# Six transpose banks for the mixed rows, their loads moved up, a stacked state update and later mapped rows in a one-core decoder step

## The chip, the cores and the metric

The kernel runs on one core of one Trainium2 chip. The metric is the device time of one execution in microseconds (us). Before the change it is 1812.33 us, the median of three runs (1810.74 to 1819.49). TensorE multiplies, VectorE (DVE), ScalarE (ACT) and GpSimd (POOL) compute elementwise, SyncE (SP) issues most DMAs, and ACT and POOL issue the others. Each engine works through its own list in order and waits on semaphores.

## What is computed

One layer of a hybrid decoder, for a prompt of 512 tokens and for 8 sequences of 4 new tokens each (32 sample rows). Width 2048.

```python
z = rms_norm(x) @ w_in                 # one projection for all three head groups
m = mLSTM(4 heads x 256)               # prompt and, with a carried state, the 8 sequences
a = sparse attention(4 x 128), keys picked by an indexer, gathered from a paged cache
c = cross-attention(4 x 128) into 256 memory tokens
mix = concat(m * silu(gate), a * silu(gate), c * silu(gate))
y = x + rms_norm(mix @ w_out)
# the carried mLSTM state of each sequence and head (T = 4 tokens):
C_new = a * C + einsum('bhs,bhse,bhsd->bhed', w_s, v, k)      # 256 x 256
n_new = a * n + einsum('bhs,bhsd->bhd', w_s, k)
h = (s @ v + a_inter * C q) / max(|den|, exp(-m_t))
```

## The kernel before

All data are float32. A projection tile is 512 columns wide and is done in 8 chunks. For each chunk ACT copies the weights to a rounded 32-bit half `w_hi`, POOL subtracts to get the rest `w_lo`, and TensorE multiplies three ways (hi by hi, lo by hi, hi by lo; L443 to L445, for the sample rows L431 and L432). A chunk is 28 matmuls of 512 columns. Other work is woven in: each engine's generators are stepped once or twice a chunk ("hosted" pieces). Four parts matter here, in order of time.

**Mapped rows.** For each sample row 256 keys are picked by top-k on DVE (L871 to L873); `vector_physical` (L875) turns them into rows of the paged cache, ending in L892/L893. `tensor_physical` (L904) waits for that (`phys_ready`), transposes the result (L908) and waits until DVE has copied it (L899, `phys_u_ready`). POOL's gathers wait for the same copy. TensorE has this piece behind chunk `MAP_AT` of the main run of tiles; the gathers begin `CK0 = MAP_AT + 2` pieces in.

**The four mLSTM heads.** After the last projection tile `tensor_mlstm_head` runs for h = 0 to 3. Inside a head come four score products (L1754), each followed by `side(0)` and `side(1)`. Beside head 0 that is the preparation of the sample state (L2109, then L2116 on TensorE; `vector_mlstm_s_prep` on DVE). Beside heads 1 to 3 each `side` is one *pair* p (one sample head and one sequence) of `tensor_mlstm_s`; 32 pairs in all, the last 8 run alone behind head 3 (I call them the tail).

**A pair.** On TensorE: the update matmuls (L2150) put v weighed by w times k into `S_UPD`; then S_OUT, the product with the turned state (L2155); then TURN, the four transposes of the next state block (L2132). On ACT: the turned state is copied out of PSUM (L2173, L2174), and S_OUT waits for it. On DVE: `weigh_values` (L2184) for the pair after, then the new state (L2194), for which the next pair's update matmuls wait, since there is one `S_UPD` bank. SP loads state blocks seven pairs ahead (L1979) and stores each new one (L1985). After the eighth pair of a head DVE normalises the output rows (L1854 to L2204), and TensorE waits for L2204.

**The mixed rows.** `mix` lies in DRAM as four blocks of 128 prompt rows and one of 32 sample rows, 2048 wide. Each is loaded (L212), turned on TensorE in groups of four transposes (L284) through the two banks `ps_a` and `ps_b`, taken as `x_hi` by ACT (L304) and as `x_lo` by DVE (L316). There are four groups to a block, 20 in all. Two blocks fit in `y_buf`; SP loads the first two behind the last head (`sync_y_early`), the others when buffers come free. Then comes the output projection (L443 again), the end of the program.

Of the kernel before, what the change touches and what calls it, by code (L numbers as in the profile page):

```python
# [4 lines left out]
def hybrid_decoder_step(nc, I, C, O):  # L5
# [65 lines left out]
    with ctx:  # L71
# [37 lines left out]
        with pro:  # L109
# [16 lines left out]
                        "qs_ready", "ot_copied", "mixed_s", "cmax", "ps_ready", "mixed_c",  # L126
                        "sm_ready", "scv_ready", "ks_scaled", "bc_copied", "qspr_ready", "pws_ready",
# [3 lines left out]
                        "g_exp", "g_ln", "g_we", "g_cols", "cexp", "gate_c_ready", "scv_silu", "sw_exp",),  # L131
# [27 lines left out]
        x_loaded = [sem("x_loaded0"), sem("x_loaded1")]  # L159
        rstd_ready, consts_in = sem("rstd_ready"), sem("consts_in")  # L160
# [39 lines left out]
        def rows_buffer(u):  # L200
            return x_in[:, u % 2, :] if u < NU_NORM else y_in(u)
# [4 lines left out]
        def sync_rows(sp, u0, u1):  # L206
            for u in range(u0, u1):
                if u >= 2:
                    sp.wait_ge(rows_turned, NGRP * (u - 1))
                if 2 <= u < NU_NORM:  # L210
                    sp.wait_ge(squares_done, u - 1)
                sp.dma_start(rows_buffer(u)[0:unit_rows[u], :], unit_source(u)).then_inc(x_loaded[u % 2], 16)  # L212
# [56 lines left out]
        def tensor_turn(pe, u):  # L269
            n = unit_rows[u]  # L270
            pe.wait_ge(x_loaded[u % 2], 16 * (u // 2 + 1))
            for j in range(NGRP):
                g = NGRP * u + j
                if u < NU_NORM:
                    if g >= 2:
                        pe.wait_ge(row_scaled, g - 1)
                else:
                    pe.wait_ge(lo_taken, g - 1)
                if j:
                    yield  # L280
                bank = (ps_a, ps_b)[g % 2]
                for i in range(TG):
                    k = j * TG + i
                    last = nc.tensor.transpose(bank[:, i * n:(i + 1) * n], rows_buffer(u)[0:n, k * P:(k + 1) * P],  # L284
                                               ident[0:n, 0:n])
                last.then_inc(rows_turned, 1)
            yield

        def scalar_take_hi(act, u):
            n = unit_rows[u]  # L290
            if u == NU_NORM:
                act.wait_ge(chunk_used, CH * N_Y0)
                act.wait_ge(sn_out, 32)
                for i in range(NCR):
                    act.wait_ge(cst_out[i], 16 * len(range(i, HB, NCR)))
            for j in range(NGRP):
                g = NGRP * u + j
                if u < NU_NORM:
                    src = turned[:, g % 2, 0:TG * n].rearrange("p (k r) -> p k r", k=TG)
                    act.wait_ge(row_scaled, g + 1)  # L300
                else:
                    src = (ps_a, ps_b)[g % 2][:, 0:TG * n].rearrange("p (k r) -> p k r", k=TG)
                    act.wait_ge(rows_turned, g + 1)
                nc.scalar.copy(unit_dest(u, j * TG, TG)[0], src).then_inc(hi_taken, 1)  # L304
                if j == NGRP - 1 and u < NU_NORM:
                    scalar_square(act, u)
                yield

        def vector_take_lo(dve, u):
            n = unit_rows[u]  # L310
            for j in range(NGRP):
                g = NGRP * u + j
                bank = (ps_a, ps_b)[g % 2][:, 0:TG * n].rearrange("p (k r) -> p k r", k=TG)
# [70 lines left out]
        def scalar_hi(act, n, c, w=TN):  # L384
            j = CH * n + c
            if not (isinstance(n, int) and j < 2):
                act.wait_ge(chunk_used, j - 1)
            scalar_load(act, n, c + 2)
# [1531 lines left out]
        k_ns = rows_of(part(xh_free, XN, [MW]), R)  # L1920
        n_in8 = rows_of(part(xh_free, XN + MW, [H, MD]), NB)
# [8 lines left out]
        assert XT + MD + 3 * H * R <= KT * (S + 2 * R)  # L1930
# [12 lines left out]
        vwb = rows_of(part(w_raw[:, RAWS - 1, :, :].rearrange("p k n -> p (k n)"), 0, [2, MD]), R)  # L1943
# [3 lines left out]
        (sm_in, sconv_out, hist_in, sx_turned, ks_turned, ks_copied, s_gate, s_added, late_in,  # L1947
            ctt, ct_copied, inter_done, vwb_ready, u_done, upd_done, hs_done, sn_done, sn_copied) = (
            sem(n) for n in ("sm_in", "sconv_out", "hist_in", "sx_turned", "ks_turned", "ks_copied", "s_gate",
            "s_added", "late_in", "ctt", "ct_copied", "inter_done", "vwb_ready", "u_done",  # L1950
# [3 lines left out]
        sn_out, hs_out, spread_set = sem("sn_out"), sem("hs_out"), sem("spread_set")  # L1954

        def sync_mlstm_s(sp):
# [5 lines left out]
            sp.wait_ge(s_added, 1)  # L1962
# [37 lines left out]
        def vector_mlstm_s_prep(dve):  # L2000
            half = 5 * MW // 2
            dve.wait_ge(sm_in, 48)
            nc.vector.tensor_tensor(out=s_nat[:, 0:half], in0=s_nat[:, 0:half], in1=s_low, op=ALU.add).then_inc(s_added, 1)
# [29 lines left out]
            yield  # L2033
            dve.wait_ge(*at("bc_copied"))
# [31 lines left out]
        def scalar_mlstm_s_prep(act):  # L2066
# [8 lines left out]
            for u in range(2):  # L2075
                act.wait_ge(ks_turned, u + 1)
                act.wait_ge(sconv_out, 16 * NB)
                nc.scalar.copy(k_ns[:, u * 512:(u + 1) * 512], (S_TURN, S_UPD)[u][0:R, :]).then_inc(ks_copied, 1)
# [4 lines left out]
        def tensor_mlstm_s_prep(pe):  # L2083
# [29 lines left out]
            pe.wait_ge(ks_copied, 2)  # L2113
# [22 lines left out]
        def tensor_mlstm_s(pe):  # L2136
            pe.wait_ge(*at("qspr_ready"))
            pe.wait_ge(spread_set, 1)
            tensor_state_turn(pe, 0)
            for p in range(HB):  # L2140
# [19 lines left out]
                if b == NB - 1:  # L2160
                    pe.wait_ge(upd_done, p + 1)
                    nc.tensor.matmul(S_UPD[0:NB, 0:MD], w_b[:, h, :], k_ns[:, h * MD:(h + 1) * MD],
# [16 lines left out]
        def vector_mlstm_s(dve):  # L2179
            def weigh_values(p):  # L2180
                h, b = p // NB, p % NB
                if p >= 2:
                    dve.wait_ge(u_done, p - 1)
                nc.vector.tensor_scalar(vwb[:, p % 2, :], s_nat[:, 2 * MW + h * MD:2 * MW + (h + 1) * MD],  # L2184
                                        w_b[:, h, b:b + 1], None, ALU.mult).then_inc(vwb_ready, 1)
# [33 lines left out]
        y_in = lambda u: y_buf[:, u % 2, :]  # L2219
        (gp_in, res_in, y_part, y_var, y_std, y_ready, y_out) = (  # L2220
            sem(n) for n in ("gp_in", "res_in", "y_part", "y_var", "y_std", "y_ready", "y_out"))

        def sync_y_early(sp):
# [3 lines left out]
            sync_rows(sp, NU_NORM, NU_NORM + 2)  # L2227
            sp.dma_start(g_post, I["norm_post"][0:1, :].broadcast_to([P, D])).then_inc(gp_in, 16)

        def sync_y_in(sp):  # L2230
            sp.wait_ge(sn_out, 32)
            for i in range(NCR):
                sp.wait_ge(cst_out[i], 16 * len(range(i, HB, NCR)))
            sync_rows(sp, NU_NORM + 2, NU_ALL)
# [20 lines left out]
        def scalar_y(act):  # L2255
            act.wait_ge(y_var, 1)
            nc.scalar.activation(y_root, y_st, ACT.Sqrt).then_inc(y_std, 1)

        def vector_y(dve):
# [25 lines left out]
            nc.vector.tensor_scalar(y_st, y_st, 1.0 / D, RMS_EPS, ALU.mult, ALU.add).then_inc(y_var, 1)  # L2285
            dve.wait_ge(y_std, 1)
# [14 lines left out]
        MAP_AT = 3  # L2301
# [339 lines left out]
```

## Time and profile before

| what | value |
|---|---|
| median of 3 runs | 1812.33 us (1810.74 to 1819.49) |
| the profiled execution, its own time | 1813.49 us |
| its span in the profile | 1811.8 us |
| TensorE busy | 1654.8 us, 91% |
| DVE busy | 826.4 us, 46% |
| ACT, POOL busy | 543.8 us (30%), 677.0 us (37%) |
| the 16 DMA engines | 249.02 MB, mean 137 GB/s |

Times in the profile are microseconds from the start of the span. A row of the timeline is: start, duration, engine, line, operation, output and inputs, count, and in brackets how long the engine had been idle and what released it. The duration of a matmul contains the depth of the pipeline, so matmuls in a row begin closer together than their durations say; the distance between starts is the pace. PEclk is the granted TensorE clock, as a share of 2.4 GHz: 1.00, or 0.50 for 1.2 GHz. A float32 matmul appears as two instructions in the trace (x4 is two matmuls).

### The profile page before, as it was taken

To read this page: it belongs to the slowest core of one execution; us is meant where nothing else is said; L and a number is where in the kernel's file an instruction comes from. 1 tells how busy PE (TensorE), PEld (TensorE's weight loads), DVE (VectorE), ACT (ScalarE), POOL (GpSimd) and SP (SyncE) were. 2 spreads that over 40 slices of the span, in tenths; PEclk is the share of its full clock that TensorE was granted. 3 is DMA by queue.
4 is the path that set the end of the run, shared out by engine and by line. 5 is a ranking of instruction groups with operands and counts; after the bars stand their busy time and mean duration, and the time that the engine had idled before them with its cause. 6 is when DMAs were issued, how large, how long until landed. Compare 5 with 4: busy or idle time off the path is not lost.

```text
span 1811.8 us, 20893 instructions
## 1 busy us (share of the span) xinstructions
PE 1654.8 (91%) x7745; PEld 1255.4 (69%) x7745; DVE 826.4 (46%) x1357; ACT 543.8 (30%) x858; POOL 677.0 (37%) x446
## 2 busy tenths in 40 slices
PE   6899999999999699998999999997849888799995
PEld 4677775577898577786688878776435555477774
DVE  6500010299999555865384347222045445401114
ACT  5512223222222143222423332323223333312221
POOL 3655531133333466674454445322101111033331
PEclk8999999999999799999999999999858789799997
DMA  5545531233234468667353634358734423632222
GB/s 211 165 115 146 158 107 45 64 108 110 90 99 122 163 202 274 197 193 233 107 151 114 203 104 148 117 89 164 241 80 145 129 92 99 236 123 82 81 85 107
DMA packets 143861, 249.02 MB, mean 137 GB/s; under 512 B 32741, under 2 KB 65449, under 8 KB 140485
## 3 DMA queue, kind: packets, MB, share of 16 engines
q10 hardware_dynamic: 66928, 122.86, 23.2%
q1 hardware_dynamic: 60202, 73.02, 12.8%
q0 software_dynamic: 16640, 51.92, 9.8%
q8 instruction: 58, 0.95, 0.2%
q14 instruction: 33, 0.27, 0.1%
HBM read 204.09 MB, written 43.66 MB: 137 GB/s over the span
## 4 chain that ended last, share of the span: by engine, by line
PE 70%; DVE 19%; DMA 5%; ACT 3%; issue 1%; POOL 1%; ACTq 1%; DVEq 0%; SPq 0%; POOLq 0%
PE acc L443 11%; PE acc L445 11%; PE acc L444 11%; DVE arena L872 4%; DVE arena L873 4%; DVE keep L871 4%; PE acc L431 3%; PE acc L432 3%; PE acc L439 3%; PE acc L441 3%; PE ps_c L1068 3%; PE acc L440 3%; PE acc L2150 2%; PE ps_c L2155 2%; DMA w_raw<-in_w_in 2%; PE acc L1765 1%
## 5 line engine op out<-in xcount | busy, mean ns | idle before, releaser
L394 POOL TENSOR_TENSOR w_lo<-w_raw,w_hi 128x1024 fp32r<-128x1024 f32 (+1 forms) x200 | 467.0, 2335 | 805.6 <-ACT w_hi L390 805.4
L443 PE MATMUL acc<-w_hi,x_hi 128*128 128x512 f32 (+1 forms) x1216 | 475.0, 391 | 12.2 <-POOL w_lo L394 11.1
L445 PE MATMUL acc<-w_hi,x_lo 128*128 128x512 f32 (+1 forms) x1216 | 465.5, 383 | 0.0
L444 PE MATMUL acc<-w_lo,x_hi 128*128 128x512 f32 (+1 forms) x1216 | 464.8, 382 | 0.0
L390 ACT CAST w_hi<-w_raw 128x1024 fp32r<-128x1024 f32 (+1 forms) x200 | 204.2, 1021 | 764.1 <-PE acc L432 705.0
L443 PEld LDWEIGHTS acc<-w_hi,x_hi 128*128 128x128 f32 x1216 | 230.3, 189 | 77.4 <-issue 17.6
L445 PEld LDWEIGHTS acc<-w_hi,x_lo 128*128 128x128 f32 x1216 | 229.7, 189 | 45.2
L444 PEld LDWEIGHTS acc<-w_lo,x_hi 128*128 128x128 f32 x1216 | 230.2, 189 | 42.3 <-issue 0.7
L431 PE MATMUL acc<-w_hi,x_hi 128*64 128x512 f32 (+1 forms) x368 | 141.5, 386 | 0.0
L432 PE MATMUL acc<-w_lo,x_hi 128*64 128x512 f32 (+1 forms) x368 | 141.1, 384 | 0.0
L439 PE MATMUL acc<-x_hi,w_hi 128*128 128x512 f32 x256 | 105.3, 411 | 0.0
L441 PE MATMUL acc<-x_lo,w_hi 128*128 128x512 f32 x256 | 100.5, 393 | 0.0
L440 PE MATMUL acc<-x_hi,w_lo 128*128 128x512 f32 x256 | 100.4, 392 | 0.0
L2270 DVE TENSOR_TENSOR arena<-arena (+1 forms) x16 | 14.0, 887 | 177.2 <-ACT arena L476 177.2
L958 POOL DMA_INDIRECT arena<-in_cache_attn_k,keep x64 | 67.1, 1049 | 19.5 <-issue 19.5
L871 DVE MAX8 keep<-arena 32x8 f32<-32x2052 f32 x32 | 73.2, 2286 | 1.1
L872 DVE FIND_INDEX8 arena<-keep,arena 32x8 uint32<-32x2052 f32 x32 | 72.9, 2277 | 0.0
L873 DVE MATCH_REPLACE8 arena<-keep,arena 32x2052 f32<-32x2052 f32 x32 | 72.6, 2268 | 0.0
L958 POOL DMA_INDIRECT arena<-in_cache_attn_v,keep x64 | 66.7, 1043 | 14.4 <-issue 11.0
L432 PEld LDWEIGHTS acc<-w_lo,x_hi 128*64 128x64 f32 x368 | 49.5, 135 | 31.6 <-issue 0.4
L695 DVE COPY head_rows<-ps_c 128x512 f32<-128x512 f32 x1 | 0.7, 694 | 153.0 <-PE ps_b L685 153.0
L431 PEld LDWEIGHTS acc<-w_hi,x_hi 128*64 128x64 f32 x368 | 49.5, 135 | 23.6 <-issue 0.2
(446 smaller groups left out, 2178.9 us busy)
## 6 DMA issues: line engine op xcount, KB each, us to landing
w_raw<-in_w_in ACTq DMA_DIRECT2D x136, 512.0 KB, 3.7
w_raw<-in_w_out ACTq DMA_DIRECT2D x32, 512.0 KB, 3.6
z_prompt<-z_tile ACTq DMA_DIRECT2D x52, 256.0 KB, 2.7
arena<-z_prompt SPq DMA_DIRECT2D x4, 2088.0 KB, 10.6
w_raw<-in_w_mem_kv ACTq DMA_DIRECT2D x16, 512.0 KB, 4.2
arena<-q_sample POOLq DMA_DIRECT2D x32, 256.0 KB, 4.1
w_raw<-in_w_in ACTq DMA_DIRECT2D x16, 300.0 KB, 3.0
x_in<-in_x_prompt SPq DMA_DIRECT2D x4, 1024.0 KB, 5.1
```

The costliest lines, as they stand in the source:

```text
L390: nc.scalar.copy(w_hi[:, c % 2, :, 0:w], w_raw[:, c % RAWS, :, 0:w]).then_inc(chunk_hi, 1)
L394: nc.gpsimd.tensor_tensor(out=w_lo[:, c % 2, :, 0:w], in0=w_raw[:, c % RAWS, :, 0:w], in1=w_hi[:, c % 2, :, 0:w].bitcast(F32), op=ALU.subt ...
L431: nc.tensor.matmul(acc[m][0:2 * R, 0:w], xs, wh, start=first, stop=False)
L432: last = nc.tensor.matmul(acc[m][0:2 * R, 0:w], xs, wl, start=False, stop=end)
L439: nc.tensor.matmul(acc[m][:, :], wh, xh, start=first, stop=False)
L440: nc.tensor.matmul(acc[m][:, :], wl, xh, start=False, stop=False)
L441: last = nc.tensor.matmul(acc[m][:, :], wh, xl, start=False, stop=end)
L443: nc.tensor.matmul(acc[m][:, 0:w], xh, wh, start=first, stop=False)
L444: nc.tensor.matmul(acc[m][:, 0:w], xh, wl, start=False, stop=False)
L445: last = nc.tensor.matmul(acc[m][:, 0:w], xl, wh, start=False, stop=end)
L871: dlink(nc.vector.max(top8, score))
L872: dlink(nc.vector.max_index(sel_idx[:, 8 * i:8 * i + 8], top8, score))
```

## The change

It has three parts.

1. **Mixed rows.** `rows_buffer` gives each of the five blocks a buffer of its own, `turn_bank` turns the groups over six PSUM banks, and a group waits only for the `x_lo` six groups back. SP issues all four prompt blocks in `sync_y_early`, ahead of the post-norm weights, the last state load and the stores of the tail; the sample block follows when its rows are stored. Before the first group TensorE waits for `c_copied` and `hs_done`. ACT's wait for the state stores moves to the second chunk of the first output tile.
2. **State update.** The keys, weighed values and weights are split in a rounded half and a rest, stacked four high on 128 partitions ([hi, hi, lo, lo] against [hi, lo, hi, lo]), so that one rounded matmul over 128 rows gives all four products that the float32 matmul over 32 rows gave. DVE makes the stacks: `vector_split_keys` once, beside head 0, and three instructions instead of one in `weigh_values`. L2116's wait becomes a wait for the split.
3. **Mapped rows.** `MAP_AT` goes from 3 to 5, and the pieces that hang on it move two chunks.

Some semaphores become points of shared ones, with the same order.

```diff
@@ rows_buffer, sync_rows, tensor_turn
-            return x_in[:, u % 2, :] if u < NU_NORM else y_in(u)
+            return x_in[:, u % 2, :] if u < NU_NORM else mix_rows[u - NU_NORM]
+        def turn_bank(u, g):
+            return (ps_a, ps_b)[g % 2] if u < NU_NORM else MIX_BANKS[g % len(MIX_BANKS)]
-                if u >= 2:
+                if 2 <= u < NU_NORM:
                     sp.wait_ge(rows_turned, NGRP * (u - 1))
+            if u == NU_NORM:
+                pe.wait_ge(c_copied, 2 * H)
+                pe.wait_ge(hs_done, H)
-                    pe.wait_ge(lo_taken, g - 1)
+                    pe.wait_ge(lo_taken, g - len(MIX_BANKS) + 1)
@@ vector_mlstm_s_prep, tensor_mlstm_s_prep
+        def vector_split_keys(dve):
+            for u in range(2):
+                cols, bank = slice(u * 512, (u + 1) * 512), (S_TURN, S_UPD)[u]
+                dve.wait_ge(ks_copied, u + 1)
+                hi = k_stack[0:R, cols]
+                nc.vector.tensor_copy(k_stack[R:2 * R, cols], hi)
+                dlink(nc.vector.tensor_tensor(out=k_stack[2 * R:3 * R, cols], in0=bank[0:R, :], in1=hi.bitcast(F32), op=ALU.subtract))
+                last = nc.vector.tensor_copy(k_stack[3 * R:4 * R, cols], k_stack[2 * R:3 * R, cols])
+            last.then_inc(reached("ks_split"), 1)
...
-            pe.wait_ge(ks_copied, 2)
+            pe.wait_ge(*at("ks_split"))
@@ tensor_mlstm_s, vector_mlstm_s
-                    last = nc.tensor.matmul(S_UPD[:, e * MD:(e + 1) * MD], vwb[:, p % 2, e * P:(e + 1) * P],
-                                            k_ns[:, h * MD:(h + 1) * MD], start=True, stop=True)
+                    last = nc.tensor.matmul(S_UPD[:, e * MD:(e + 1) * MD], v_stack[:, p % 2, e * P:(e + 1) * P],
+                                            k_stack[:, h * MD:(h + 1) * MD], start=True, stop=True)
@@ sync_y_early, sync_y_in
-            sync_rows(sp, NU_NORM, NU_NORM + 2)
+            sync_rows(sp, NU_NORM, NU_NORM + MT)
...
+            sync_rows(sp, NU_NORM + MT, NU_ALL)
             for i in range(NCR):
                 sp.wait_ge(cst_out[i], 16 * len(range(i, HB, NCR)))
-            sync_rows(sp, NU_NORM + 2, NU_ALL)
@@ main
-        MAP_AT = 3
+        MAP_AT = 5
```

What DVE does for two pairs beside a head, before (L2184 weighs the values, L2194 makes the new state):

```order
L2184 TENSOR_SCALAR w_raw<-between,keep_m 32x256
L2194 SCALAR_TENSOR_TENSOR mem_kv<-mem_kv,z_tile,acc 128x512
L2184 TENSOR_SCALAR w_raw<-between,keep_m 32x256
L2194 SCALAR_TENSOR_TENSOR mem_kv<-mem_kv,z_tile,acc 128x512
```

and the weighing of one pair in the changed kernel:

```order
L2218 TENSOR_SCALAR x_hi<-between,keep_m 32x256
L2219 SCALAR_TENSOR_TENSOR x_hi<-between,keep_m,x_hi 32x256
L2221 COPY x_hi<-x_hi 64x256
```

Each pair's weighing, which stands in front of the state of the pair before it, has grown from one instruction to three, each of which waits for the one before.

SP's list behind the last head, before:

```order
L212 DMA arena<-mix_prompt 128x2048 x2
L2228 DMA arena<-in_norm_post 128x2048
L1985 DMA out_s_C<-mem_kv 128x2x256
L1979 DMA between<-in_state_mlstm_C 128x2x256
L1985 DMA out_s_C<-mem_kv 128x2x256 x3
```

and in the changed kernel:

```order
L222 DMA arena<-mix_prompt 128x2048 x4
L2265 DMA arena<-in_norm_post 128x2048
L2015 DMA out_s_C<-mem_kv 128x2x256
L2009 DMA between<-in_state_mlstm_C 128x2x256
L2015 DMA out_s_C<-mem_kv 128x2x256 x3
```

Two more loads of 1024 KB stand ahead of the load of the last state block.

DVE at the end of the mapping, before:

```order
L893 TENSOR_TENSOR arena<-arena 32x256
L899 CAST keep<-ps_c 128x64
L670 TENSOR_TENSOR arena<-arena,keep 128x64
L671 TENSOR_TENSOR arena<-arena,keep 128x64
L672 TENSOR_TENSOR arena<-arena,keep 128x64
```

and in the changed kernel the same copy, now L913:

```order
L688 TENSOR_TENSOR arena<-arena 128x4x16
L689 TENSOR_TENSOR arena<-arena 128x4x16
L913 CAST keep<-ps_c 128x64
L684 TENSOR_TENSOR arena<-arena,keep 128x128
L685 TENSOR_TENSOR arena<-arena,keep 128x128
```

The copy that TensorE and POOL wait for has moved behind twelve rotation instructions of 128x64.

## Rows read from the trace of the kernel before

**Rows 1.** The page's chain that ended last, its shares by line.

```profile
PE acc L443 11%; PE acc L445 11%; PE acc L444 11%; DVE arena L872 4%; DVE arena L873 4%; DVE keep L871 4%; PE acc L431 3%; PE acc L432 3%; PE acc L439 3%; PE acc L441 3%; PE ps_c L1068 3%; PE acc L440 3%; PE acc L2150 2%; PE ps_c L2155 2%; DMA w_raw<-in_w_in 2%; PE acc L1765 1%
```

**Rows 2.** Timeline around the mapped rows, TensorE and DVE.

```profile
579.82 0.40 PE L443 MATMUL acc<-w_hi,x_hi 128*128 128x512 f32 x1
...
604.83 0.42 PE L908 MATMUL ps_c<-ident,arena 32*128 32x32 f32 x2 [18.47 <-DVE arena L893]
...
605.29 0.23 DVE L899 CAST keep<-ps_c 128x64 uint32<-128x64 f32 x1 [0.51 <-PE ps_c L908]
...
607.28 0.22 DVE L675 TENSOR_TENSOR arena<-arena 128x64 f32<-128x64 f32 x1
```

**Rows 3.** Timeline beside head 0: L2116 and DVE's last score product.

```profile
1357.93 1.06 PE L2116 MATMUL acc<-z_tile 128*32 128x32 f32 x16
...
1358.11 0.29 DVE L1812 SCALAR_TENSOR_TENSOR arena<-ps_a,arena 128x128 f32<-128x128 f32 x1 [0.92 <-PE ps_a L1754]
```

**Rows 4.** Groups of DVE by form: busy us, mean ns of one.

```profile
L1868 DVE TENSOR_TENSOR between<-between 32x256 f32<-32x256 f32 x4 | 1.7, 413 | 0.1
L2274 DVE COPY z_tile<-arena 32x512 f32 x3 | 1.2, 416 | 0.0
```

**Rows 5.** The chain in order of time, one pair of the tail: start, length.

```profile
1541.75 0.59 PE acc L2132 x4
1542.34 1.06 PE acc L2150 x4
1543.39 0.99 PE ps_c L2155 x4
```

**Rows 6.** Timeline: ACT and DVE of pairs in the tail; the last TURN's weights.

```profile
1542.38 0.59 ACT L2173 COPY z_tile<-acc 128x512 f32<-128x512 f32 x1 [1.95 <-PE acc L2132]
1542.86 0.20 ACT L2174 COPY z_tile<-z_tile 128x2 f32<-128x2 f32 x1
...
1543.43 0.75 DVE L2194 SCALAR_TENSOR_TENSOR mem_kv<-mem_kv,z_tile,acc 128x512 f32<-128x512 f32 x1 [1.63 <-PE acc L2150]
1544.10 0.34 DVE L2184 TENSOR_SCALAR w_raw<-between,keep_m 32x256 f32<-32x256 f32 x1
...
1552.20 0.42 PEld L2132 LDWEIGHTS acc<-ident,between 128*128 128x128 f32 x4 [0.41 <-DMA between<-in_state_mlstm_C]
```

**Rows 7.** Timeline beside head 2: a score product and its use on DVE.

```profile
1494.95 1.46 PE L1754 MATMUL ps_a<-between 128*128 128x384 f32 x4
...
1496.52 0.56 DVE L1812 SCALAR_TENSOR_TENSOR arena<-ps_a,arena 128x384 f32<-128x384 f32 x1 [0.79 <-PE ps_a L1754]
```

**Rows 8.** DMA issues (count, KB, us to landing), issued at 1540.6 and 1541.8.

```profile
arena<-in_norm_post SPq DMA_DIRECT2D x1, 1024.0 KB, 9.9
...
between<-in_state_mlstm_C SPq DMA_DIRECT2D x1, 256.0 KB, 10.1
```

**Rows 9.** Windows: length, busy of PE, PEld, DVE, ACT, POOL, then PEclk, DMA share, GB/s.

```profile
1544.00:1545.00 1.00, 1.00 (x7) 0.52 (x5) 0.43 (x2) 0.00 (x0) 0.00 (x0) 1.00 1.00 418
...
1557.00:1558.00 1.00, 0.00 (x0) 0.00 (x0) 0.75 (x5) 0.08 (x1) 0.00 (x0) 0.58 0.04 5
...
1587.00:1588.00 1.00, 1.00 (x4) 0.81 (x3) 0.00 (x0) 0.00 (x0) 0.12 (x1) 0.56 0.93 377
```

**Rows 10.** Timeline of the mixed rows, from the last L2204 to the output tile.

```profile
1559.19 1.12 PE L284 MATMUL ps_a<-ident,arena 128*128 128x128 f32 x4 [3.77 <-DVE between L2204]
...
1560.10 1.06 PE L284 MATMUL ps_b<-ident,arena 128*128 128x128 f32 x4
1561.61 0.59 ACT L304 CAST x_hi<-ps_a 128x512 fp32r<-128x512 f32 x1 [4.53 <-DMA mix_sample<-between]
...
1562.22 0.69 DVE L316 TENSOR_TENSOR x_lo<-ps_a,x_hi 128x512 fp32r<-128x512 f32 x1 [3.09 <-ACT x_hi L304]
1562.83 0.68 DVE L316 TENSOR_TENSOR x_lo<-ps_b,x_hi 128x512 fp32r<-128x512 f32 x1
...
1583.84 0.76 PE L443 MATMUL acc<-w_hi,x_hi 128*128 128x512 f32 x1 [0.73 <-issue]
```

More of the change, by code:

```diff
@@ L159, in hybrid_decoder_step @@
         x_loaded = [sem("x_loaded0"), sem("x_loaded1")]
+        mix_in = [(x_loaded[i], 16 * (len(range(i, NU_NORM, 2)) + 1)) for i in range(2)]
+        mix_in += [(sem(f"mix_in{i}"), 16) for i in range(2, MT + 1)]
         rstd_ready, consts_in = sem("rstd_ready"), sem("consts_in")
@@ L277, in tensor_turn @@
                 else:
-                    pe.wait_ge(lo_taken, g - 1)
+                    pe.wait_ge(lo_taken, g - len(MIX_BANKS) + 1)
                 if j:
                     yield
-                bank = (ps_a, ps_b)[g % 2]
+                bank = turn_bank(u, g)
                 for i in range(TG):
@@ L312, in vector_take_lo @@
                 g = NGRP * u + j
-                bank = (ps_a, ps_b)[g % 2][:, 0:TG * n].rearrange("p (k r) -> p k r", k=TG)
+                bank = turn_bank(u, g)[:, 0:TG * n].rearrange("p (k r) -> p k r", k=TG)
                 hi, lo = unit_dest(u, j * TG, TG)
@@ L387, in scalar_hi @@
                 act.wait_ge(chunk_used, j - 1)
+            if isinstance(n, int) and n == N_Y0 and c == 1:
+                for i in range(NCR):
+                    act.wait_ge(cst_out[i], 16 * len(range(i, HB, NCR)))
             scalar_load(act, n, c + 2)
@@ L2002, in vector_mlstm_s_prep @@
             dve.wait_ge(sm_in, 48)
-            nc.vector.tensor_tensor(out=s_nat[:, 0:half], in0=s_nat[:, 0:half], in1=s_low, op=ALU.add).then_inc(s_added, 1)
+            nc.vector.tensor_tensor(out=s_nat[:, 0:half], in0=s_nat[:, 0:half], in1=s_low, op=ALU.add).then_inc(reached("s_added"), 1)
             dve.wait_ge(sm_in, 64)
@@ L2077, in scalar_mlstm_s_prep @@
                 act.wait_ge(sconv_out, 16 * NB)
-                nc.scalar.copy(k_ns[:, u * 512:(u + 1) * 512], (S_TURN, S_UPD)[u][0:R, :]).then_inc(ks_copied, 1)
+                nc.scalar.copy(k_stack[0:R, u * 512:(u + 1) * 512], (S_TURN, S_UPD)[u][0:R, :]).then_inc(ks_copied, 1)
             act.wait_ge(*at("bc_copied"))
@@ L2161, in tensor_mlstm_s @@
                     pe.wait_ge(upd_done, p + 1)
-                    nc.tensor.matmul(S_UPD[0:NB, 0:MD], w_b[:, h, :], k_ns[:, h * MD:(h + 1) * MD],
+                    nc.tensor.matmul(S_UPD[0:NB, 0:MD], w_stack[:, h, :], k_stack[:, h * MD:(h + 1) * MD],
                                      start=True, stop=True).then_inc(sn_done, 1)
@@ L2218, in hybrid_decoder_step @@
         y_rows = lambda m: y_t[:, m, :]
[L2219 to L2221 removed]
+        mix_rows = [y_buf[:, 0, :], y_buf[:, 1, :], place(M0, [D]), place(M0 + D, [D]), place(0, [D], R)]
+        MIX_BANKS = (ps_a, ps_b, acc[0], acc[1], acc[2], ps_c)
+        (gp_in, res_in, y_part, y_ready, y_out) = (
+            sem(n) for n in ("gp_in", "res_in", "y_part", "y_ready", "y_out"))
         def sync_y_early(sp):
@@ L2255, in scalar_y @@
         def scalar_y(act):
-            act.wait_ge(y_var, 1)
-            nc.scalar.activation(y_root, y_st, ACT.Sqrt).then_inc(y_std, 1)
+            act.wait_ge(*at("y_var"))
+            nc.scalar.activation(y_root, y_st, ACT.Sqrt).then_inc(reached("y_std"), 1)
         def vector_y(dve):
```

52 lines of the change are left out of this document (33 added, 19 removed).

## The prediction

> **What bounds the kernel now.** I read the chain that ended last first: three fifths of its listed shares are the projection matmuls, the top-k on DVE follows, and L2150 and L2155 have 2% each [rows 1]. None of the projection work changes, so the question is what happens at three places where something else ends last: the mapped rows, the pairs and the mixed rows. For these I read the timeline, the chain in order of time and the windows with their clock.
>
> At the mapped rows TensorE stands idle for 18.47 us, up to 604.83, for DVE's L893 [rows 2]. In a pair of the tail TURN, update and S_OUT take 0.59 + 1.06 + 0.99 = 2.64 us [rows 5]. ACT copies the turned state from 1542.38 to 1543.06, and S_OUT begins at 1543.39 [rows 5, 6]: the update matmuls lie beside ACT's copy and end only 0.3 us behind it. In the mixed rows 24.65 us pass from 1559.19 to the output tile at 1583.84 [rows 10].
>
> **The sum** is made against the profiled execution's own 1813.5 us.
>
> *Mapped rows.* The chunk from 579.82 ends where the idle time begins, at 586.36, and holds 28 matmuls [rows 2]: 6.4 us without the edges. Two such chunks move into the 18.5 us hole: -12.8; 5.7 us of hole stay. DVE's twelve rotations now stand ahead of the copy L899; they ran from about 605.43 to 607.50 [rows 2] and their data is in by then, so the copy comes 2.0 us later: +2.0. The gathers keep their distance to the copy. At their end TensorE waits for a softmax step on DVE that now stands behind four index accumulations; no row prices the new order, the ends are 0 and a chunk, 6.4, and I take +1.5. Together **-9.3**.
>
> *Preparation beside head 0.* L2116 began at 1357.93, and DVE's last score product ends at 1358.40 [rows 3]. Behind it DVE now makes the key stack, twice a copy, a subtraction and a copy of 32x512. The copy of that form takes 0.42 [rows 4]; for the subtraction, which reads PSUM, I take the mixed rows' pace for 512 columns, 0.61 [rows 10]. Twice (0.36 + 0.64 + 0.36) is 2.7 us, and TensorE resumes at 1361.2: +3.3. An idle stretch costs the clock: TensorE, idle from 1555.4 on [rows 10], was granted 0.58 in the second from 1557 [rows 9]. I add 1.5 for slow matmuls behind it. **+4.8** (3.3 to 6.5).
>
> *Pairs beside heads 1 to 3.* The update matmul over 256 columns becomes one rounded pass. The projection's rounded 512 columns have a pace of about 0.23 (6.4 us for 28), so 256 take about 0.12, and the update of a pair about 0.3 with its first weight load, instead of 1.06. On DVE the weighing goes from 0.34 [rows 6] to 0.37 + 0.44 + 0.29 = 1.1: the old instruction, one of L1868's form (0.41) and a copy of half of L2274's columns [rows 4], each with about 0.03 for the link. Bounds: 0.85 and 1.4. What is late next is DVE. Between two score products, from the end of L1754: L1812 0.1 + 0.47 [rows 7], weighing 1.1, the new state 0.7 and 0.1 to TensorE [rows 6], then the second pair's update 0.3, S_OUT 0.99, TURN 0.59. That is 4.35 us, against two pairs of 2.63, 5.26, before: -0.9. It is -1.0 for the shorter L1812 after it, about -0.95 at the first score product, where ACT's copy is late, and -0.8 at the last, where the new state and a weighing stand before the normalisation. -3.65 a head, three heads: **-11.0** (-7 to -14 over the weighing's bounds). L2162's saving is worth nothing: TensorE then waits for L2204.
>
> *Tail.* Alone, a pair would be TURN, ACT's copy and S_OUT, 0.65 + 0.72 + 0.06 + 0.99 = 2.42, so 0.2 less for each. But the last state load was issued at 1541.8 and landed 10.1 us later, at 1551.9, and the last TURN needed it at 1552.20 [rows 6, 8]: 0.3 us of margin. The norm weights, issued a microsecond before it, landed at 1550.5, the state 1.4 us behind them, in order of issue [rows 8]. Now two more loads of 1.05 MB stand ahead. At the 418 GB/s of that stretch [rows 9] they take 5.0 us, so the block lands at 1556.9 and the last TURN starts 4.7 us later than before, whatever the shorter pairs save. TensorE has then been idle for over 5 us and is at 1.2 GHz [rows 9]; TURN and S_OUT (1.6 us in all) may double, some 1.2 of it on the path. **+5.9**. The stores behind the load drain in about 4 us, before the sample rows' store, which took from 1559.5 to 1561.6 [rows 10] and still gates ACT.
>
> On the order of DMAs the Trainium skill (DMA: Bandwidth & Descriptors, Queues, rings and completion order) says that each DMA engine takes the descriptors of a ring in order, though completion is not strictly in order of issue; the landings above agree with the first half. By a looser order than that, the second rival below would hold.
>
> *Mixed rows.* Call the end of L2204 zero. TensorE starts at 0.06 as now. ACT waits for the sample store, as now, until 2.45, DVE starts at 3.1 [rows 10]. Six groups can be turned meanwhile; one takes 0.91 at the low clock [rows 10], so TensorE has them at 5.5 and never waits for a bank. A group of four transposes at full clock takes 0.59 [rows 5], and DVE has a pace of 0.61 [rows 10]: DVE ends the sixteen full groups at 3.1 + 16 x 0.61 = 12.9, the four small ones at 14, the output tile at 14.4, if the clock is back to 2.4 GHz after some 6 us of work. If it stays at 1.2, TensorE needs 16 x 0.91 + 4 x 0.5 = 16.6, and the tile starts at 17.6. I take 14.4: **-10.3** (-7 to -10.5).
>
> *Output tile.* It began at 1.2 GHz and was granted more only in the second from 1587 [rows 9]: 4.1 us at twice the pace, 2 us lost. If TensorE has worked without a gap before it, this goes: **-1.9** (0 to -2).
>
> Sum: -9.3 + 4.8 - 11.0 + 5.9 - 10.3 - 1.9 = -21.8, and 1813.5 - 21.8 = 1791.7. The median was 1.2 below the profiled execution; I forecast **1791 us**. Terms at their bounds, not all to one side, give 1783 to 1800.
>
> **Rivals.**
>
> *The last state block is not held up.* Loads of different blocks may overlap more than their order of issue says. Then the tail gives -1.2 instead of +5.9: 1784. For it: that the loads share one queue in full order is read from two landings only. Against: the engines were full from 1544 [rows 9] and the landings came in order.
>
> *The mapped rows give nothing.* TensorE is 11 us earlier against DVE for the rest of the projection, and any DVE chain with less slack than that takes it back as new waits for the prompt's attention. For it: the hole shows that DVE set the time there. Against: that DVE chain ends at 604.8 in both, and nothing else in the chain's list is DVE work of the prompt [rows 1]. 1791 + 9 = 1800.
>
> *The clock stays down in the mixed rows.* TensorE had gaps there; if it stays at 1.2 GHz, +3.2 and +1.9, and some more in the pairs: 1797.
>
> *The update is no faster.* If the rounded matmul over 128 rows keeps the pace of the old one, the cycle of 4.35 becomes 5.1, and the heads give -1.5: 1800.
>
> *Slower than before.* Shorter updates leave TensorE waiting for DVE or ACT about 0.4 us in each pair, where it had none [rows 5]. If these gaps bring the clock down to 1.2 GHz through heads 1 to 3, S_OUT and TURN (1.58) cost up to as much again in each of the 24 pairs, 38 us, less the slack of about 10 us in which DVE's chain is the later one anyway, and the score products more. That gives 1791 + 28 = 1819. It decides from about 80% of the pairs at the low clock. Against it: gaps of 0.4 us are far shorter than the 1.6 us after which the grant had fallen at 1557 [rows 9].
>
> **How the numbers follow.** The forecast (1786 to 1797) has 0.50; the free state block 0.15; the mapped rows lost 0.15; the low clock in the mixed rows 0.12; the update no faster 0.04; slower 0.04. The range runs from 1781, below the second case, to 1803, above the two at 1800. A measurement of this kernel can tell about 0.5%, 9 us, from no change, so faster means under 1803.3: the first four cases but for a tail of the mapped rows' case, 0.87; within 0.5% 0.09; slower 0.04.
>
> **What would show it.** In the changed profile: L922 (once L908) idle about 6 us instead of 18.5, and its copy some 2 us behind it; a new wait of about 3 us of L2116's successor for DVE's key stack; the update matmuls at about a quarter of 1.06 us a pair, with TensorE now waiting for DVE's new state beside the heads, and two pairs with their score product some 0.9 us shorter; one wait of 5 to 6 us of the last TURN for the state load; the mixed rows in 14 to 18 us with DVE back to back, and the output tile at full clock from its start. The forecast fails if the mapped chunk's gain comes back as waits for DVE before 1300, if the state block lands in time, or if the clock stays low in the pairs.

## The result: a smaller gain than forecast, at the edge of what can be told

The changed kernel takes 1806.94 us (median of 13 runs, 1797.09 to 1815.44), the kernel before 1816.63 us in the same session (13 runs, 1809.3 to 1823.47). The ratio is 0.9949, 95% interval 0.9932 to 0.9965: about 9 us faster, where some 22 were forecast, and outside the range given. (The forecast stood against the first three runs of the kernel before, median 1812.33 us; all 13 have 1816.63.) In the profiled execution, 1806.94 us with a span of 1805.3, TensorE is busy for 1626.5 us (before 1654.8), DVE for 855.4 (826.4), ACT 542.0, POOL 678.3.

The stages of both profiled executions, in us, cut at the same instructions. "Sample rows turned" is TensorE's first transposes for the sample state, beside head 0 (L2117, before L2086); "split wait" is L2147 (before L2116); a norm wait is where TensorE has waited for the end of a head's normalisation (L2240, before L2204). The last two columns are from an experiment below.

| stage | before | after | before_conv_late | after_conv_late |
|---|---|---|---|---|
| start to sample rows turned | 1332.9 | 1339.65 | 1321.57 | 1321.06 |
| to the split wait | 25.0 | 28.7 | 25.0 | 28.7 |
| to the norm wait of head 1 | 52.7 | 52.2 | 52.5 | 52.3 |
| of head 2 | 55.8 | 47.4 | 55.7 | 47.4 |
| of head 3 | 50.9 | 48.0 | 50.8 | 48.0 |
| tail, to the first mixed row | 42.0 | 48.1 | 42.0 | 47.2 |
| to the output tile | 24.65 | 13.6 | 24.65 | 13.6 |
| to the end | 228.0 | 227.7 | 227.9 | 228.8 |

From the second row on, the changed kernel is 13.3 us faster, near the forecast for those stages. In the first row it is 6.75 us slower, where 9.3 us less were forecast. So the miss lies ahead of 1340 us.

**The mapped rows.** The timeline after, TensorE, DVE and POOL, answers to [rows 2]:

```profile
593.28 2.50 DVE L907 TENSOR_TENSOR arena<-arena 32x256 f32<-32x256 f32 x1
...
599.49 2.60 DVE L907 TENSOR_TENSOR arena<-arena 32x256 f32<-32x256 f32 x1
602.50 0.41 DVE L907 TENSOR_TENSOR arena<-arena 32x256 f32<-32x256 f32 x1
...
593.10 2.40 POOL L408 TENSOR_TENSOR w_lo<-w_raw,w_hi 128x1024 fp32r<-128x1024 f32 x1 [3.95 <-ACT w_hi L404]
599.48 2.34 POOL L408 TENSOR_TENSOR w_lo<-w_raw,w_hi 128x1024 fp32r<-128x1024 f32 x1 [3.98 <-ACT w_hi L404]
...
607.91 0.42 PE L922 MATMUL ps_c<-ident,arena 32*128 32x32 f32 x2 [10.01 <-DVE arena L907]
610.16 0.80 PE L457 MATMUL acc<-w_hi,x_hi 128*128 128x512 f32 x1 [1.83 <-DVE keep L913]
```

TensorE's idle time fell from 18.47 to 10.01 us, not to 5.7. Two DVE instructions (L907, an addition at the end of `vector_physical`) that take 0.41 elsewhere took 2.50 and 2.60, each beginning where POOL's `w_lo` of a moved chunk begins, or 0.2 us behind it, and ending up to 0.3 us behind its end. The copy L913 begins 1.97 us after the transpose L922, where it was 0.46 before: 1.5 us, and 2.0 were forecast. TensorE resumes 4.6 us later than before with two chunks (12.8) more done: a lead of 8.2 us.

**Then the lead goes.** Waits of TensorE between 600 and 1350 us (total, times, longest), after, the longest and those that differ:

```profile
PE acc L2117 <- DVE between L2035: 19.2, 1, 19.2
PE acc L457 <- POOL w_lo L408: 16.9, 1, 16.9
PE ps_c L922 <- DVE arena L907: 10.0, 1, 10.0
...
PE ps_a L1207 <- ACT arena L1227: 3.0, 1, 3.0
PE acc L453 <- DVE arena L1022: 2.1, 1, 2.1
...
PE ps_a L1246 <- DVE keep L1016: 1.9, 1, 1.9
```

and before, the rows that answer to them, but for the hole of [rows 2]:

```profile
PE acc L2086 <- DVE between L2005: 16.7, 1, 16.7
PE acc L443 <- POOL w_lo L394: 9.1, 1, 9.1
...
PE ps_a L1193 <- ACT arena L1213: 1.4, 1, 1.4
...
PE ps_a L1232 <- DVE keep L1002: 1.2, 1, 1.2
...
PE ps_a L1232 <- DVE arena L1008: 0.6, 1, 0.6
```

L1246 and L453 wait for the sample rows' softmax steps on DVE, L1207 for ACT's copy of the turned prompt rows: each takes a part of the lead. Counted chunk by chunk at ACT's copy of the weights, the lead is 9.7 us at 619 us, 5.6 at 640, 5.3 from 911 to 1177, 2.7 at 1212 and -5.5 at 1239. (At 562, ahead of the mapped rows, this execution was already 1.2 us ahead.) The largest row, the wait at the end of the first stage, is in both kernels: behind the last sample rows of the cross-attention stand a store, a load of 10 us and a second load, then the sums that L2117 waits for. TensorE comes to that wait 6 us late already. What made it late is the second row, a weight chunk near 1238 us whose `w_lo` came late because its load did. The chain in order of time, after:

```profile
1201.93 36.81 DMA w_raw<-in_w_in
1238.77 1.05 ACT w_hi L404
```

and before:

```profile
1205.41 27.82 DMA w_raw<-in_w_in
1233.24 1.05 ACT w_hi L390
```

A weight load elsewhere takes 3.7 us. SP had begun to issue six stores of 4 KB, `out_p_conv<-small`, shortly before, at 1199.1 and 1204.2 us, made of single elements. Windows (columns as in [rows 9]) of after, then of before, from their issue on:

```profile
1199.00:1226.00 27.00, 25.90 (x128) 19.66 (x126) 6.88 (x9) 3.73 (x7) 4.76 (x2) 1.00 1.60 2
```

```profile
1204.00:1232.00 28.00, 22.55 (x105) 16.58 (x104) 6.88 (x9) 3.63 (x7) 4.82 (x2) 1.00 0.81 27
```

The DMA share, a sum of the packets' times that can exceed 1, is 1.60 and 0.81, and 2 and 27 GB/s are moved. The stores are the same in both kernels; the load that TensorE needs next fares differently behind them. SP took 15.8 us to issue the six after and 30.8 before.

**The later stages after.** Waits of TensorE from 1340 to 1600 us, those that the change brought:

```profile
PE acc L2182 <- DVE mem_kv L2230: 6.3, 6, 3.2
PE acc L2163 <- DMA between<-in_state_mlstm_C: 4.9, 1, 4.9
...
PE acc L2147 <- DVE x_hi L1980: 3.6, 1, 3.6
PE acc L2182 <- DVE between L2230: 3.1, 6, 0.6
```

The wait for the key split, for the last state block and for the new state are all there. DVE beside a head, timeline after:

```profile
1445.27 0.33 DVE L2218 TENSOR_SCALAR x_hi<-between,keep_m 32x256 fp32r<-32x256 f32 x1
1445.64 0.47 DVE L2219 SCALAR_TENSOR_TENSOR x_hi<-between,keep_m,x_hi 32x256 fp32r<-32x256 f32 x1
1446.15 0.29 DVE L2221 CAST x_hi<-x_hi 64x256 fp32r<-64x256 f32 x1
1446.47 0.75 DVE L2230 SCALAR_TENSOR_TENSOR mem_kv<-mem_kv,z_tile,acc 128x512 f32<-128x512 f32 x1
1447.13 0.61 DVE L1821 TENSOR_SCALAR arena<-ps_b,keep_m 128x384 f32<-128x384 f32 x1
```

No gaps, and a weighing of 1.2 us from start to start. The last state block, in the chain after, answers to the 10.1 us of [rows 8]:

```profile
1541.61 14.26 DMA between<-in_state_mlstm_C
1555.87 0.04 issue
1555.91 1.13 PE acc L2163 x4
```

The mixed rows and the output tile, which answer to [rows 10] and to the last row of [rows 9]; the chain, then two windows:

```profile
1567.07 8.47 DVE x_lo L327 x14
...
1576.01 1.60 issue
1577.61 0.47 PE acc L457
```

```profile
1577.00:1579.00 2.00, 1.39 (x6) 1.22 (x7) 0.57 (x4) 0.86 (x1) 1.06 (x1) 0.99 0.93 291
1579.00:1582.00 3.00, 3.00 (x8) 2.32 (x8) 0.00 (x0) 0.00 (x0) 1.32 (x1) 0.50 0.99 393
```

DVE works back to back (14 groups in 8.47 us, 0.605 each). The tile begins at full clock and falls to 1.2 GHz at 1579, 1.4 us later.

### The profile page after: what moved, and what is told of

Its sections match the earlier page's. It is cut to its first block, busy times and chain, and to the rows that moved or that the text cites. A ratio compares the mean times of both kernels' runs of the same rounds, so it can differ in the third digit from the quotient of the medians.

```text
span 1805.3 us, 20833 instructions
## 1 busy us (share of the span) xinstructions
PE 1626.5 (90%) x7677; PEld 1241.3 (69%) x7677; DVE 855.4 (47%) x1430; ACT 542.0 (30%) x858; POOL 678.3 (38%) x446
## 4 chain that ended last, share of the span: by engine, by line
PE 64%; DVE 22%; DMA 7%; ACT 3%; issue 2%; POOL 1%; ACTq 1%; SPq 0%; DVEq 0%; POOLq 0%
PE acc L457 11%; PE acc L459 11%; PE acc L458 11%; DVE arena L886 4%; DVE arena L887 4%; DVE keep L885 4%; PE acc L445 3%; PE acc L446 3%; PE acc L453 3%; PE ps_c L1082 3%; PE acc L455 3%; PE acc L454 3%; DMA w_raw<-in_w_in 2%; PE acc L1779 2%; DMA arena<-z_prompt 1%
## 5 line engine op out<-in xcount | busy, mean ns | idle before, releaser
L453 PE MATMUL acc<-x_hi,w_hi 128*128 128x512 f32 x256 | 105.9, 414 | 2.1 <-DVE arena L1022 2.1
L446 PEld LDWEIGHTS acc<-w_lo,x_hi 128*64 128x64 f32 x368 | 49.7, 135 | 31.8 <-issue 0.8
L445 PEld LDWEIGHTS acc<-w_hi,x_hi 128*64 128x64 f32 x368 | 49.7, 135 | 23.7 <-issue 0.4
```

Of the source, the lines that this page charges most:

```text
L445: nc.tensor.matmul(acc[m][0:2 * R, 0:w], xs, wh, start=first, stop=False)
L446: last = nc.tensor.matmul(acc[m][0:2 * R, 0:w], xs, wl, start=False, stop=end)
L453: nc.tensor.matmul(acc[m][:, :], wh, xh, start=first, stop=False)
```

## Experiments

Every ratio is to the kernel before, run on the same chip beside it. Kernels of one group shared a chip; medians of different groups are on different chips.

### Each part alone, and the change without one

Edits: map5_only is the kernel before with

```diff
-        MAP_AT = 3
+        MAP_AT = 5
```

stack_only and mixed_only are the kernel before with the diff's hunks of part 2 and of part 1 alone. after_map3 is the changed kernel with the line above undone.

> The kernel before with MAP_AT = 5 and nothing else of the change. As predicted: 9.3 us below the kernel before. Theory from the two traces: the idle time in front of the mapped rows is 8 us shorter (TensorE waits about 10 us for L893 and about 2 for the copy), but the lead is gone behind the store out_p_conv<-small near 1200 us, where the weight load takes 37 us against 28, so the whole is 0 to 7 us above the kernel before. Rival: the long load was a chance of one execution; then it takes about 28 us here and the whole is 3 to 6 us below.

Measured: 1815.75 us, ratio 0.9996 (0.9975 to 1.0017). The mapped rows' part gives at most 4.5 us by the interval, and nothing by the median. The trace has the same marks as after: 9.8 us idle in front of L908, a lead of 3.2 us by 1197 us, and a wait of 17.9 us for the late `w_lo`. This is the forecast's rival "the mapped rows give nothing".

> The kernel before with the stacked state update alone. Theory: L2116's successor starts about 3.5 us later against the score products, heads 1 to 3 take 11 to 12 us less, the tail is no longer (the last state load is not behind two more loads), 0 to 2 us less: 7 to 10 us below the kernel before. Rival (part of the 12 us gained beside the heads was a spell of low clock in the one execution of before): 3 to 5 us below.

Measured: 1805.15 us, ratio 0.9954 (0.9939 to 0.9969), 8.3 us below, as the theory has it and not the rival.

> The kernel before with the mixed rows' part alone (six banks, five buffers, early loads). Theory: the mixed rows take 13.6 to 14.4 us instead of 24.65, the output tile still begins slow for some us, and the last state block lands some 5 us later: tail +4.5 to +6. In sum 5 to 7 us below the kernel before.

Measured: 1814.92 us, ratio 1.0003 (0.9989 to 1.0017). Less than either figure: the interval ends at 2 us below. The profiled execution has the tail's wait (4.4 us) and mixed rows of 13.6 us, but came to the sample state 5.9 us later than before; nothing of part 1 runs ahead of that point. Its own stages are 4.3 us shorter in that trace; why the times show none of it stays open here.

> The changed kernel with MAP_AT = 3. If the mapped rows' part cost 0 to 7 us in the whole, as the two traces show at 1332 us: 0 to 7 us below the changed kernel, 12 to 17 us below the kernel before. If it is worth the 9.3 us of the prediction and another part lost its gain: about 9 us above the changed kernel, level with the kernel before.

Measured: 1803.73 us, ratio 0.9948 (0.9931 to 0.9965), the same as the changed kernel's 0.9949. Dropping part 3 loses nothing.

### The element stores moved out of the way

The runs of one kernel spread over 8 to 18 us, and the six profiled executions reach the sample state at 1333 (before), 1337, 1337.5 and 1339 (the other three with `MAP_AT` = 3), 1340 and 1343 us (the two with 5). To take the stores out of it, six kernels issue them behind `sync_y_in`, spread over the output projection; the output rows' sums move to `head_rows`, since they would overwrite what is stored, and in the changed kernel `sync_y_in` no longer waits for these stores:

```diff
@@ sync_conv_state, now behind sync_y_in
-            sp.wait_ge(cv_tapped, 4 * NCT)
...
+                    sp.wait_ge(chunk_used, CH * N_Y0 + 4 + 3 * (3 * half + j))
                     sp.dma_start(O["p_conv"][0, 0, j, half * MW:(half + 1) * MW].rearrange("(k p) -> p k", p=P),
@@ vector_y
-        y_sum = small[:, 32:32 + NY * (MT + 1)].rearrange("p (m n) -> p m n", m=MT + 1)
+        y_sum = head_rows[:, 0:NY * (MT + 1)].rearrange("p (m n) -> p m n", m=MT + 1)
```

> The kernel before with the six stores out_p_conv<-small issued behind sync_y_in, one every third weight chunk of the output projection, instead of all at once near 1200 us (the sums of the output rows move out of the same small tensor). Theory: these stores hold the DMA engines from 1204 to 1232 us while a weight load waits; without them the wait of 9.1 us for POOL's w_lo goes and nothing is lost under the output projection, whose load share is 0.25: 9 to 14 us below the kernel before, and a narrower spread of its runs. Rival: the stores delay weights there as well, or another load of that stretch is late in their place: 0 to 5 us below.

Measured: 1801.52 us (1797.45 to 1806.84), ratio 0.9942 (0.992 to 0.9963), 10.8 us below the kernel before. The stores cost that much where they stood, and nothing under the output projection (227.9 us in the table against 228.0). The narrower spread did not come: 9.4 us in 6 runs, against 9.1 in the 11 of the kernel before on this chip.

> The changed kernel with the same six stores moved in the same way. Theory: the mapped rows' lead, still 3 to 4 us near 1197 us, was lost because the stores came to stand where the weight load took 37 us; now it survives: 12 to 13 us below before_conv_late (that kernel with MAP_AT = 3 stands 9 below it). Rival: the lead is lost elsewhere: level with after_conv_late_map3.

Measured: 1788.5 us (1785.79 to 1788.76), ratio 0.9866 (0.9847 to 0.9886), 13.0 us below before_conv_late. The gain of the change is 4 us larger by the medians than with the stores in place, and the spread is 3 us in 5 runs instead of 18 in 13. The window that answers to the two above:

```profile
1199.00:1227.00 28.00, 27.67 (x138) 21.75 (x137) 9.73 (x13) 7.28 (x11) 7.83 (x4) 1.00 0.23 68
```

> after_conv_late with MAP_AT = 3. Theory: 3 to 4 us above after_conv_late, and about 9 us below before_conv_late (state update and mixed rows). The prediction's 9.3 us for the mapped rows would put it 9 us above after_conv_late.

Measured: 1786.37 us, ratio 0.9864 (0.9844 to 0.9884), 2 us below its partner with `MAP_AT` = 5, not above it. The theory that only the stores took the lead is wrong, and after_conv_late met its forecast by chance. The two kernels turn the sample rows at 1321.06 and 1321.08 us. The lead of the later mapping, chunk for chunk at ACT's copy of the weights, was 7.4 us at 632 us, 4.3 from 641 to 836, 1.7 at 895, 2.5 from 921 to 1177, 0.7 at 1204 and 0.2 from 1214 on. The first step has two halves: TensorE's wait for L1227 is 2.98 us instead of 1.73, and the clock falls behind the longer wait. Windows of after_conv_late and of after_conv_late_map3 that begin about with that wait's end:

```profile
635.00:640.00 5.00, 4.48 (x16) 3.57 (x17) 0.89 (x1) 3.28 (x7) 3.29 (x4) 0.66 0.42 114
```

```profile
640.00:645.00 5.00, 3.68 (x20) 2.89 (x21) 0.23 (x1) 4.17 (x9) 3.83 (x3) 1.00 0.49 138
```

The steps at 880 and 905 us are the waits for DVE's softmax of the sample rows. What is left then is no lead. The 32 sums over the gathered rows (L1082) follow that softmax, one a chunk, and with `MAP_AT` = 5 they are two chunks late. TensorE's busy time in them from 1100 to 1240 us, for `MAP_AT` = 3 and for 5:

```profile
1100.00:1240.00 140.00, 18.41 (x160) 19.41 (x160) 1.00 0.36 113
```

```profile
1100.00:1240.00 140.00, 20.84 (x182) 21.85 (x181) 1.00 0.38 119
```

A sum is 1.84 us. Two of them, 3.7 us, were still to be done by the kernel that was 2.5 us ahead in chunks; when they are, both are level.

Behind 1321 us the profiled execution with 3 is 4.7 us shorter than the one with 5: 2.1 us up to the norm wait of head 1, 1.8 in the tail, 1.1 at the end. No instruction of part 3 stands there, but the stretches at low clock lie otherwise: about the first 4 us of the tail have 0.50 with 5 and 1.00 with 3. The norm wait of head 1 comes 52.2 to 52.3 us behind the split wait in the four stacked traces with `MAP_AT` of 4 or 5, and 50.2 to 50.8 in the five with 3 (weigh_twice aside). Why the clock follows this is not shown.

### The last state block ahead of the mixed rows

```diff
@@ sync_y_early (and sync_states without its load of the last block)
+            sync_state_in(sp, HB - 1)
             sync_rows(sp, NU_NORM, NU_NORM + MT)
```

> after_conv_late with the load of the last state block issued ahead of the four loads of mixed rows in sync_y_early instead of behind them and a store. Theory: the block lands some 3 us after its issue near 1538, the last TURN waits for nothing, and the mixed rows' loads are in long before they are needed: 5 to 7 us below after_conv_late. Rival: the tail's end is set by DVE and ACT in any case: 0 to 1 us below.

Measured: 1782.2 us (1781.18 to 1783.77), ratio 0.9836 (0.9816 to 0.9855), 6.3 us below after_conv_late. Its DMA issues:

```profile
between<-in_state_mlstm_C SPq DMA_DIRECT2D x1, 256.0 KB, 2.6
```

The block lands after 2.6 us instead of 14.3, the last TURN waits for nothing, and the tail takes 41.8 us instead of 47.2; the mixed rows take 14.5 instead of 13.6. The cost of the early loads is shown.

### Parts 1 and 2 again, with the stores out of the way

> before_conv_late with the mixed rows' part alone. Theory: without the stores near 1200 the stretch up to the sample state's preparation takes the same in both, so only the part's own terms are left: mixed rows -11, the last state block late +6 to +7, the slower first pairs of the tail 0, sum -4 to -5: about 1797. Rival (mixed_only was level with the kernel before because the part itself gives nothing in the time): level with before_conv_late, 1801.5.

Measured: 1797.78 us (1794.4 to 1800.0), ratio 0.993 (0.9907 to 0.9952); before_conv_late has 1801.52 and 0.9942 on another chip. About 2 to 4 us below by ratio and medians, but the two intervals overlap, so the times alone don't exclude the rival. The trace bears out the terms: tail 48.8 instead of 42.0 (+6.8), mixed rows 13.6 instead of 24.65 (-11.1).

> before_conv_late with the stacked state update alone. Theory: key split +3.7, pairs beside heads 1 to 3 about -12, tail -1 to -1.5: 9 to 10 us below before_conv_late, about 1792. With mixed_conv_late's -4.5 that adds up to the 13 to 15 us between before_conv_late and after_conv_late(_map3).

Measured: 1792.8 us (1790.21 to 1797.74), ratio 0.9903 (0.988 to 0.9927), 7 to 9 us below before_conv_late.

> after_conv_late_c31 with MAP_AT = 3. Theory: the later mapped rows bring nothing up to 1321 us, so it is level with after_conv_late_c31, at most 2 us off, about 1781. If the later mapped rows do carry a gain to the end: 3 to 9 us above.

Measured: 1780.72 us (1778.25 to 1783.18), ratio 0.984 (0.9816 to 0.9864), against 0.9836 for `MAP_AT` = 5. Level. It is the fastest version here with part 3 left out: 26 us below the changed kernel by the medians, about 29 below the kernel before by its ratio.

### DVE as the bound of the pairs

```diff
@@ weigh_values, in after_conv_late_c31_map3
+                dlink(nc.vector.tensor_copy(v_stack[2 * R:4 * R, p % 2, :], v_stack[0:2 * R, p % 2, :]))
                 nc.vector.tensor_copy(v_stack[2 * R:4 * R, p % 2, :], v_stack[0:2 * R, p % 2, :]).then_inc(vwb_ready, 1)
```

> after_conv_late_c31_map3 with the last of the three DVE instructions of the weighing (the 64x256 copy, 0.30 us) made twice. Theory: DVE back to back is the bound of the pairs beside heads 1 to 3, so each of the 24 pairs costs 0.3 us more, while in the tail ACT's copy of the turned state is the later one: 6 to 8 us above after_conv_late_c31_map3. Rival: TensorE or ACT sets the cycle there too: 0 to 2 us above.

Measured: 1793.02 us, ratio 0.9901 (0.9879 to 0.9923), 12.3 us above. DVE is the bound beside the heads. The cost is above the forecast: 0.29 us on DVE cost 0.45 a pair. The norm waits of heads 2 and 3 stand 51.6 us behind the one before instead of 48.1 and 47.9, and the tail takes 43.6 instead of 39.7. In the cycle DVE also waits for the score product that TensorE can only begin once its own late pairs are done: 1.20 us in one such place of head 2, 0.43 without the second copy. In the stages of heads 2 and 3 together the copies are 4.6 us more of DVE work and DVE's waits 2.4 us more, 7.0 of the 7.2 us. TensorE was slower there too, granted 0.87 where it was 0.89 and 0.91 without, so how much of the 2.4 us is the loop and how much the clock is not told apart. The same holds for the tail, where no cost was expected and 3.9 us came: its clock was 0.85 against 0.95.

### One chunk instead of two

> after_conv_late_c31_map3 with MAP_AT = 4, one chunk instead of two moved in front of the mapped rows. Theory: one w_lo of POOL falls into the rotations of L907 and one of them takes about 2.5 us instead of 0.41; TensorE's idle time there is 18.4 - 6.4 + 2.1, about 14, and L922 starts some 2 us later than with MAP_AT = 3. The lead of 4 to 5 us is gone before 1320, and the whole is level with both neighbours, 1779 to 1783. Rival (DVE was slower there for another reason, such as TensorE's matmuls): no rotation, or several, above 0.5 us, and not beside w_lo.

Measured: 1784.1 us, ratio 0.982 (0.9794 to 0.9845). Its DVE and POOL, and TensorE behind them:

```profile
593.10 2.44 DVE L907 TENSOR_TENSOR arena<-arena 32x256 f32<-32x256 f32 x1
...
592.87 2.40 POOL L408 TENSOR_TENSOR w_lo<-w_raw,w_hi 128x1024 fp32r<-128x1024 f32 x1 [3.89 <-ACT w_hi L404]
...
605.48 0.42 PE L922 MATMUL ps_c<-ident,arena 32*128 32x32 f32 x2 [14.19 <-DVE arena L907]
```

(The expectation calls L907 a rotation; it is the last addition of `vector_physical`.) One chunk moved, one long L907, beside its `w_lo`, and 14.19 us of idle time where 14 were expected. In no trace without a moved chunk is an L907 long; with two moved two are, or, in map5_only, one and its neighbour L892 with 2.31 us. The lead of 4.6 us is 2.6 at 929 us and 1.1 at 1211, and at the sample state it is gone (1319.1 against 1318.9 us).

## Why the prediction missed, step by step

**Mapped rows (-9.3).** This is the step that failed, twice. The idle time was read as if DVE's part could not change: "5.7 us of hole stay" left out that each moved chunk brings POOL work beside DVE's additions L907. Each cost 2.1 to 2.2 us of DVE, 4.3 in all; the copy cost 1.5 where 2.0 were forecast. The trace of the kernel before held the case, two chunks earlier:

```profile
581.56 3.04 POOL L394 TENSOR_TENSOR w_lo<-w_raw,w_hi 128x1024 fp32r<-128x1024 f32 x1 [3.99 <-ACT w_hi L390]
...
582.37 2.31 DVE L670 TENSOR_TENSOR arena<-arena,keep 32x64 f32<-32x64 f32 x1
...
585.50 0.21 DVE L670 TENSOR_TENSOR arena<-arena,keep 32x64 f32<-32x64 f32 x1
```

The SBUF — State Buffer page of the Trainium skill (Who interferes with whom, and SBUF: two separate sides) has this case: a DVE instruction with two SBUF inputs and a GpSimd instruction that reads SBUF exclude each other for a whole instruction. L670 and L907 are of that kind, and the trace agrees: 2.31 us instead of 0.21 and 2.50 instead of 0.41.

With the 2.42 us of `w_lo` before, two L907 would have grown by 2.0 us each, and the forecast of the hole would have been 9.7 us; measured 10.0. The second failure is larger: what was left, 8.2 us in the trace, was taken as a gain of the whole program, less 1.5 us for a softmax step. In the pair without the stores all but 2.5 us were gone by some 920 us, in waits for DVE and ACT of 3 us and less each and in slow matmuls behind them, which the page's list of the chain, cut off at 1%, could not show; and those 2.5 us were no gain, since the pieces that `MAP_AT` moves along are work of TensorE's that is only postponed (two sums, 3.7 us). The rival that said so had 0.15 and a price of 1800; against it stood that "nothing else in the chain's list is DVE work of the prompt". That was no evidence: a chain that ends last does not show by how little the next one is shorter.

**What was not seen at all.** The stores near 1200 us cost the kernel before 10.8 us. In the changed kernel the spread shrank with them (18 us to 3); in the kernel before it did not, and what makes it there stays open. The stores are not part of the change, but a shift of some microseconds decides how long the load behind them takes (27.8 and 36.8 us in the two profiled executions; waits of 9.1 to 11.3 us in the four traces with `MAP_AT` = 3 and 16.9 and 17.9 in the two with 5). With one profile a kernel, whether that difference is due to the position or to chance stays open; SP's issue of the six stores took 30.2 to 31.2 us in those four traces and 14.6 and 15.8 in those two. By the times the position makes no difference beyond 3 to 5 us, the width of the intervals, since `MAP_AT` gives nothing either way. The change as a whole gives 9 us with the stores in place and 13 without; the two intervals overlap (6 to 12 us, and an estimate of 10 to 16 from the runs of the two kernels), so the 4 us are not certain.

**Preparation (+4.8).** 3.6 us of wait for the split (forecast 3.3: the copies took 0.42, the subtractions 0.68) and 3.7 us in the stage. The slow clock's 1.5 is not in it but in the next stage: TensorE was granted 0.50 until 1374 us, 5.7 us behind the end of the wait, and before only until 1359, 1.2 us behind it. At half the pace that is an estimate of 2.2 us, and part of why head 1 gave only 0.5.

**Pairs beside heads 1 to 3 (-11.0).** -0.5, -8.4 and -2.9, -11.7 in sum. The sum is right by luck, for a reason that was not in it: between the norm waits of heads 1 and 2 lie 55.6 to 55.8 us in all five traces without part 2 and 47.3 to 49.7 in those with it (51.6 in weigh_twice), against 50.8 and some 48 for head 3. The kernel before has a spell at low clock there. Window of before, then of after:

```profile
1429.00:1445.00 16.00, 15.69 (x33) 7.20 (x34) 3.79 (x8) 4.63 (x10) 0.00 (x0) 0.51 0.87 279
```

```profile
1429.00:1445.00 16.00, 13.69 (x50) 6.88 (x50) 11.46 (x30) 5.20 (x11) 0.00 (x0) 0.89 0.37 118
```

Why the spell went with part 2 is not shown. At one clock (head 3: 0.90 and 0.89) a head gives some 2.9 us, not 3.65. The weighing is 1.2 and not 1.1.

**Tail (+5.9).** +6.1, or +5.2 with the stores late: the state load takes 14.26 us. The mechanism was right, and after_conv_late_c31 takes 5.3 of it away. Of the 1.2 us that the pairs were to save only 0.2 came (41.8 in stack_conv_late against 42.0; 39.7 in after_conv_late_c31_map3, where the tail's clock was 0.95 and not 0.87), since the first pair waits 3.2 us for the new state behind two weighings and the normalisation, 1.7 before.

**Mixed rows (-10.3).** 13.6 us instead of 24.65, -11.1. ACT waited for the sample rows' store and DVE set the pace, as said.

**Output tile (-1.9).** -0.3 in the last stage. TensorE was to work "without a gap before it"; there are 1.6 us of issue ahead of the tile, and the low clock only moved: the tile's first 4.0 us had it before, and after it has some 3.2 us that begin 1.4 us into the tile.

**The sum.** Forecast -21.8. The stages behind the sample state gave -13.3 where -12.5 were forecast, with errors in the heads and the output tile that cancel. The mapped rows gave 0 instead of -9.3. That makes the change worth about -13, which is what it measures without the element stores. With them it measures 9; where the rest goes, and why part 1 alone gives nothing there, stays open.

## What to carry to other kernels

A hole in front of TensorE is worth what the next chain allows: look for the same engine's small waits in the rest of the program before counting it, and look at what the moved work does on POOL while DVE fills the hole. A DMA of single elements belongs where nothing is waited for, and a load whose consumer is near belongs ahead of large loads in its queue. When runs of one kernel spread by more than the effect, find the stage that spreads, and try to take it away first; it worked for the changed kernel alone.

## What the runs showed that was not expected

Six stores of 4 KB in single elements, 6144 of them, kept the DMA engines at a share of 0.81 and 1.60 for 27 us with 2 to 27 GB/s moved; a 512 KB load beside them took 28 to 37 us instead of 3.7, though it is in another queue. POOL's subtraction of two SBUF operands stretched a DVE instruction of 0.34 or 0.41 us to 2.3 to 2.6, in each of the five traces in which a moved chunk brought them together. And an instruction of 0.29 us added to the bound engine cost 0.45 a pair, with the clock's share in it not told apart.
